# Embedding normalisation of a hybrid decoder step: from feature rows to token tiles, with eight PSUM banks for the transposes

## What is computed

```python
def layer_norm(x, g, b):
    xf = x.astype(jnp.float32)
    mu = jnp.mean(xf, -1, keepdims=True)
    var = jnp.mean(jnp.square(xf - mu), -1, keepdims=True)
    return ((xf - mu) * lax.rsqrt(var + LN_EPS) * g + b).astype(x.dtype)
...
xp = layer_norm(jnp.concatenate([meta, x_prompt], axis=1), emb_ln_g, emb_ln_b)
xs = layer_norm(x_sample, emb_ln_g, emb_ln_b)
...
proj = jnp.einsum('btd,dc->btc', x, w_in).astype(f32)      # first step of a layer's token mixer
```

## Time and profile before

| | us |
|---|---|
| runs before: median (lowest to highest of 3) | 1586.23 (1585.19 to 1592.24) |
| the profiled execution, its own time | 1596.57 |
| its span, first to last instruction | 1594.3 |
| TensorE busy | 1505.8 |
| VectorE busy | 923.2 |
| ScalarE busy | 686.4 |
| opening: start of the span to the first matmul of group 1 | 70.4 |

### The profile page before, as it was taken

The page is one execution under the profiler, slowest core; times in us unless marked ns, Lnnn a source line. Parts: engine busy times, 40 slices in busy tenths (PEclk is TensorE's granted clock), DMA queues, the critical chain, the costliest instruction groups (busy, mean ns, idle before and its releaser), DMA issues.

```text
span 1594.3 us, 30590 instructions
## 1 busy us (share of the span) xinstructions
PE 1505.8 (94%) x12047; PEld 1221.0 (77%) x12047; DVE 923.2 (58%) x1499; ACT 686.4 (43%) x1067; POOL 89.1 (6%) x86
## 2 busy tenths in 40 slices
PE   3899999999999999999989999999999999999995
PEld 2677878777788888878767887877777888887874
DVE  5767775546755555533476777555585555553334
ACT  4655552343743434322365555333264343432224
POOL 0011112110000000000001111111000000000000
PEclk7999999999999999999999999999899999999998
DMA  7222233221223222232333322321212323222321
GB/s 210 71 82 81 81 86 103 83 87 62 80 80 105 79 94 90 72 85 86 107 93 86 82 81 81 108 82 54 88 61 80 104 80 105 79 80 75 96 73 57
DMA packets 175042, 138.19 MB, mean 87 GB/s; under 512 B 5064, under 2 KB 169192, under 8 KB 174776
## 3 DMA queue, kind: packets, MB, share of 16 engines
q1 hardware_dynamic: 168192, 113.46, 23.8%
q0 software_dynamic: 5408, 18.60, 4.2%
q10 hardware_dynamic: 1372, 5.16, 0.9%
HBM read 125.12 MB, written 12.07 MB: 86 GB/s over the span
## 4 chain that ended last, share of the span: by engine, by line
PE 75%; DVE 10%; ACT 8%; DVEq 3%; issue 2%; ACTq 1%; DMA 1%; SPq 0%
PE ACC L561 62%; ACT X L973 2%; ACT XH L972 1%; PE OT L705 1%; PE SCR L735 1%; DVE Fb L1460 1%; PE OT L757 1%; DVE WL L1380 1%; PE SCR L618 1%; PE SCR L806 1%; DVE X L1430 1%; ACT WH L946 1%; PE SCR L561 1%; PE OT L561 1%; DVE B L1466 1%
## 5 line engine op out<-in xcount | busy, mean ns | idle before, releaser
L561 PE MATMUL ACC<-XH,WH 128*128 128x280 f16 x2304 | 483.6, 288 | 8.4 <-DVE XL L1435 6.6
L561 PE MATMUL ACC<-XL,WH 128*128 128x280 f16 x2304 | 483.1, 287 | 0.0
L561 PE MATMUL ACC<-XH,WL 128*128 128x280 f16 x2304 | 482.7, 287 | 0.0
L1380 DVE SCALAR_TENSOR_TENSOR WL<-stage,WH 128x2048 f16<-128x2048 f32 (+1 forms) x108 | 228.8, 2119 | 128.0 <-ACT WH L946 121.7
L561 PEld LDWEIGHTS ACC<-XH,WH 128*128 128x128 f16 x2304 | 227.8, 101 | 70.6 <-DVE XL L1435 8.4
L561 PEld LDWEIGHTS ACC<-XL,WH 128*128 128x128 f16 x2304 | 228.8, 99 | 54.4 <-issue 0.9
L561 PEld LDWEIGHTS ACC<-XH,WL 128*128 128x128 f16 x2304 | 229.1, 99 | 53.4
L946 ACT ACTIVATE WH<-stage 128x2048 f16<-128x2048 f32 (+1 forms) x108 | 190.5, 1764 | 98.4 <-PE ACC L561 71.9
L561 PE MATMUL ACC<-shared,WH 128*128 128x280 f16 x1320 | 214.7, 283 | 2.0 <-issue 2.0
L561 PEld LDWEIGHTS ACC<-shared,WH 128*128 128x128 f16 x1320 | 128.8, 98 | 31.2 <-issue 3.1
L561 PE MATMUL ACC<-shared,WL 128*128 128x280 f16 x660 | 139.8, 283 | 0.0
(11 more groups left out here) (262 smaller groups left out, 2004.0 us busy)
## 6 DMA issues: line engine op xcount, KB each, us to landing
stage<-in_w_in_dram SPq DMA_DIRECT2D x64, 512.0 KB, 5.3
stage<-in_w_a_dram SPq DMA_DIRECT2D x44, 512.0 KB, 4.3
stage<-in_w_b_dram SPq DMA_DIRECT2D x44, 512.0 KB, 4.4
stage<-in_w_down_dram SPq DMA_DIRECT2D x32, 384.0 KB, 3.5
stage<-in_w_down_dram SPq DMA_DIRECT2D x32, 320.0 KB, 3.9
out_dram<-shared POOLq DMA_DIRECT2D x16, 512.0 KB, 3.9
stage<-in_w_o_dram SPq DMA_DIRECT2D x16, 512.0 KB, 3.9
shared<-in_state_ret_dram POOLq DMA_DIRECT2D x8, 512.0 KB, 4.6
```

What stands on the lines that cost most here:

```text
L561: last = mm(dst(h), lhs, x[:, xk + k, tokens(h)], start=begin, stop=end)
L1380: stt(out=wl[:, 0:width], in0=stage[:, s, 0:width], scalar=W_SCALE, in1=wh[:, 0:width], op0=ALU.mult, op1=ALU.subtract).then_inc(w_lo[s], 1)
```

## The change

The first layer norm is computed on the token tiles as they lie, before the transposes. The three whole prompt tiles come in three DMAs, each with a semaphore of its own. For each tile VectorE takes mean and variance along the free dimension (`token_sums`: two `bn_stats` over 512 elements, one `bn_aggr`), ScalarE the deviation of one column (`token_deviation`), and VectorE normalises the tile in place (`token_norm`). TensorE transposes the normalised tiles into eight PSUM banks, one for each feature row (`left_bank`); all of ACC, OT and SCR are free at that time. Tiles 0 to 2 hold the left half. VectorE applies gain and bias straight out of the bank into X (`opening_rows`), ScalarE copies X to XH (`left_high`), VectorE makes XL as before.

The right half's transposes (tiles 2 to 4, `transpose_right`) are woven between the matmuls of the left half, into four banks used twice; ScalarE applies gain and bias out of these banks into XH and X (`right_rows`). The right half's matmuls, all four tiles, wait once for all eight XL pairs.

The squares, the reductions over feature rows, the matmuls with ones, and the mean and variance rows go away for these two halves; they stay for all later layer norms. The parameters are fetched in ten DMAs of norm parameters (both layers in one) and four of convolution parameters; the norm parameters are transposed ahead of tile 2, the convolution parameters with the last right row. ScalarE's function table is loaded ahead of all DMAs, and the large tables are fetched behind the deviation of the last tile. ScalarE's `split_hi` and VectorE's `split_lo` of the next unit keep their place in the program ahead of VectorE's last two XL pairs of the right half.

The diff, cut: without declarations of semaphores, index changes, and the removed bodies of `transpose_params`, `transpose_x`, `start_jobs` and `first_rows`:

```diff
+        SUM6, MEAN_VAR, RSD = (B[:, a:b] for a, b in ((0, 12 * TT5), (12 * TT5, 14 * TT5), (14 * TT5, 15 * TT5)))
...
+        def norm_column(n, o, m):
+
+            at = m + 8 * o if n == 0 else 16 + 32 * ((n - 1) % 2) + 16 * o + 8 * ((n - 1) // 2) + m
+            return par[:, 2 * P + at:2 * P + at + 1]
...
+        left_bank = (ACC[:, 0, 0, :], ACC[:, 1, 0, :], OT[:, 1, :], ACC[:, 0, 1, :], ACC[:, 1, 1, :], OT[:, 0, :], SCR[:, 0, :], SCR[:, 1, :])
+        right_bank = (OT[:, 1, :], ACC[:, 0, 1, :], ACC[:, 1, 1, :], SCR[:, 1, :]) * 2
+        norms_bank = SCR[:, 1, LEFT_TILES * P:LEFT_TILES * P + ROWS2]
+        conv_bank = SCR[:, 1, T - RIGHT0:T - RIGHT0 + DEPTH * ROWS01]
...
-            sp.dma_start(XT[:, 1:4, :], xp[first:first + 3 * P, :].rearrange("(i p) d -> p i d", p=P)).then_inc(x_in[1], 16)
-            sp.dma_start(XT[0:TAIL, 4, :], xp[first + 3 * P:SEQ, :]).then_inc(x_in[2], 16)
-            sp.dma_start(XT[TAIL:R5, 4, :], x_sample.rearrange("b t d -> (b t) d")).then_inc(x_in[2], 16)
+            for i in range(1, 4):
+                sp.dma_start(XT[:, i, :], xp[first + (i - 1) * P:first + i * P, :]).then_inc(x_in[i], 16)
+            sp.dma_start(XT[0:TAIL, 4, :], xp[first + 3 * P:SEQ, :]).then_inc(x_in[4], 16)
+            sp.dma_start(XT[TAIL:R5, 4, :], x_sample.rearrange("b t d -> (b t) d")).then_inc(x_in[4], 16)
...
-                    last.then_inc(scr_full, 1)
+            def transpose_left():
+
+                pe.wait_ge(consts_in, 16)
+                for i in range(LEFT_TILES):
+                    if i == LEFT_TILES - 1:
+                        pe.wait_ge(norms_in, 16 * N_NORM_DMAS)
+                        nc.tensor.transpose(norms_bank, rows[0:ROWS2, 2, :], ident[0:ROWS2, 0:ROWS2]).then_inc(norms_full, 1)
+                    pe.wait_ge(token_rows, i + 1)
+                    for m in range(KT):
+                        if i == LEFT_TILES - 1 and m == KT - 1:
+                            pe.wait_ge(norms_ready, 1)
+                        last = nc.tensor.transpose(left_bank[m][:, i * P:(i + 1) * P], XT[:, i, m * P:(m + 1) * P], ident)
+                        if i == LEFT_TILES - 1:
+                            last.then_inc(row_full, 1)
+
+            def transpose_right(m):
+
+                pe.wait_ge(x_ready, (2, 2, 3, 4, 5, 5, 6, 6)[m])
+                pe.wait_ge(token_rows, TT5)
+                for i in range(LEFT_TILES - 1, TT5):
+                    n, at_ = P if i < 4 else R5, i * P - RIGHT0
+                    last = nc.tensor.transpose(right_bank[m][:, at_:at_ + n], XT[0:n, i, m * P:(m + 1) * P], ident[0:n, 0:n])
+                if m == KT - 1:
+                    last.then_inc(ot_full, 2)
+                    pe.wait_ge(params_in, 16 * N_CONV_DMAS)
+                    for b in range(DEPTH):
+                        last = nc.tensor.transpose(conv_bank[:, b * ROWS01:(b + 1) * ROWS01], rows[0:ROWS01, b, :], ident[0:ROWS01, 0:ROWS01])
+                last.then_inc(row_full, 1)
+
+            def opening_units():
+
+                pairs = ((1, (acc(0), acc(1))), (2, (lambda h: OT[:, h, 0:HALF], lambda h: SCR[:, h, 0:HALF])))
+
+                def one(k, pair, h):
+                    for c in range(2):
+                        last = products(pair[1][c], pair[0], 2 * P, c * P, lambda _: k, XH, XL, k, 1, k == 0, k == KT - 1, (h,))
+                        if h == 1 and k == KT - 1:
+                            last.then_inc(acc_full, 1)
+
+                transpose_left()
+                pe.wait_ge(w_lo[0], 2)
+                for k in range(KT):
+                    if k % 2 == 0:
+                        pe.wait_ge(x_ready, k // 2 + 1)
+                    one(k, pairs[0], 0)
+                    for m in {4: (0, 1), 5: (2,), 7: (3,)}.get(k, ()):
+                        transpose_right(m)
+                pe.wait_ge(w_lo[1], 2)
+                for k in range(KT):
+                    one(k, pairs[1], 0)
+                    for m in {2: (4, 5), 5: (6, 7)}.get(k, ()):
+                        transpose_right(m)
+                pe.wait_ge(x_ready, 2 * PAIRS)
+                for pair in pairs:
+                    for k in range(KT):
+                        one(k, pair, 1)
...
-            for i in range(3):
-                transpose_x(i)
-            transpose_params()
-            norm_stats(0, 0, 1, jobs_at_start["left",][1])
-            for i in (3, 4):
-                transpose_x(i)
             for l in range(DEPTH):
-                first_group(l)
+                if l == 0:
+                    opening_units()
+                else:
+                    first_group(l)
...
+            nc.scalar.preload_act_table_set("natural_log_exp_and_others")
             act.dma_start(tab[:, 0:first_tables], consts[:, 0:first_tables]).then_inc(consts_in, 16)
-            loads = []
+            norms = [(emb_ln_g, 0), (emb_ln_b, 8), (ln1_g, 16), (ln1_b, 32), (ln2_g, 48), (ln2_b, 64),
+                     (hg_norm_g, ROW_HG), (rt_gn_g, ROW_RG), (rt_gn_b, ROW_RB), (lb_logits, ROW_LB)]
+            assert len(norms) == N_NORM_DMAS
+            for src, at_ in norms:
+                flat = src.rearrange("(k p) -> k p", p=P) if len(src.shape) == 1 else src.rearrange("l (k p) -> (l k) p", p=P)
+                act.dma_start(rows[at_:at_ + flat.shape[0], 2, :], flat).then_inc(norms_in, 16)
...
-            act.dma_start(tab[:, first_tables:n_const], consts[:, first_tables:n_const]).then_inc(tables_in, 16)
+                act.dma_start(rows[0:CONV_W * FT, l, :], conv_w[l].rearrange("j (f p) -> (j f) p", p=P)).then_inc(params_in, 16)
+                act.dma_start(rows[CONV_W * FT:ROWS01, l, :], conv_b[l].rearrange("(f p) -> f p", p=P)).then_inc(params_in, 16)
...
-            def first_rows(i):
+            def token_deviation(i):
                 n = P if i < 4 else R5
-                act.wait_ge(scr_full, jobs_at_start["x", i, 1][0])
-                f(X[:, 4:8, i * P:i * P + n], SCR[:, 0, :].rearrange("p (k t) -> p k t", k=4)[:, :, 0:n], ACT.Copy).then_inc(scr_read[0], 1)
-
-            def first_sums(h):
-                act.drain().then_inc(x_high_rows, 1)
-                act.wait_ge(x_low_rows, h + 1)
-                f(first_squares[:, :, tokens(h)], X[:, :, tokens(h)], ACT.Square).then_inc(first_sq, 1)
...
+                if i == 0:
+                    act.wait_ge(consts_in, 16)
+                act.wait_ge(token_var, i + 1)
+                f(RSD[0:n, i:i + 1], MEAN_VAR[0:n, 2 * i + 1:2 * i + 2], ACT.Ln, bias=tab[0:n, eps_at:eps_at + 1])
+                act.drain()
+                f(RSD[0:n, i:i + 1], RSD[0:n, i:i + 1], ACT.Exp, scale=-0.5).then_inc(token_rstd, 1)
+
+            def left_high(pair):
+                act.wait_ge(left_rows, pair + 1)
+                f(XH[:, 2 * pair:2 * pair + 2, tokens(0)], X[:, 2 * pair:2 * pair + 2, tokens(0)], ACT.Copy).then_inc(ln_out, 1)
+
+            def right_rows(pair):
+                for m in (2 * pair, 2 * pair + 1):
+                    act.wait_ge(row_full, KT + m + 1)
+                    src = right_bank[m][:, HALF - RIGHT0:T - RIGHT0]
+                    g, b = (norm_column(0, o, m) for o in range(2))
+                    f(XH[:, m, tokens(1)], src, ACT.Identity, scale=g, bias=b)
+                    last = f(X[:, m, tokens(1)], src, ACT.Identity, scale=g, bias=b)
+                last.then_inc(ln_out, 1)
+
+            for i in range(LEFT_TILES):
+                token_deviation(i)
+            act.wait_ge(norms_full, 1)
+            f(par[:, 2 * P:2 * P + ROWS2], norms_bank, ACT.Copy)
+            act.drain().then_inc(norms_ready, 1)
+            split_hi(0, 0, (acc_full, 1), slot=1)
+            for i in range(LEFT_TILES, TT5):
+                token_deviation(i)
+            act.dma_start(tab[:, first_tables:n_const], consts[:, first_tables:n_const]).then_inc(tables_in, 16)
+            for pair in range(PAIRS):
+                left_high(pair)
+                if pair == 1:
+                    split_hi(1, 0, (acc_full, 1), slot=2)
+            for pair in range(PAIRS):
+                right_rows(pair)
+            f(par[:, 0:DEPTH * P].rearrange("p (l c) -> p l c", l=DEPTH)[:, :, 0:ROWS01],
+              conv_bank.rearrange("p (l c) -> p l c", l=DEPTH), ACT.Copy)
             act.drain().then_inc(params_ready, 1)
-            first_sums(0)
-            split_hi(0, 0, (acc_full, 1), slot=1)
-            norm_mean(0, 0, ot0(0))
-            norm_rstd(0, 0, 0)
-            for pair in range(2):
-                norm_rows(0, 0, 0, pair)
-            for i in (3, 4):
-                first_rows(i)
-            first_sums(1)
-            for pair in range(2, PAIRS):
-                norm_rows(0, 0, 0, pair)
-            split_hi(1, 0, (acc_full, 1), slot=2)
...
+                if l:
+                    nc.scalar.preload_act_table_set("natural_log_exp_and_others")
+                    norm_mean(4 * l + 1, 1, ot0(l) + 1)
+                    norm_rstd(4 * l + 1, 2 * l, 1)
```

(72 more changed lines are left out.)

84 lines of the change are left out of this document (17 added, 67 removed).

## The result

| | before, us | changed, us |
|---|---|---|
| median of 18 runs each (lowest to highest) | 1593.06 (1585.19 to 1605.66) | 1583.73 (1576.65 to 1590.72) |
| ratio, with its 95% interval | | 0.9937 (0.9915 to 0.9958) |
| profiled execution, its own time | 1596.57 | 1584.03 |
| its span | 1594.3 | 1582.4 |
| first product of TensorE | 36.69 | 21.11 |

The change is faster by 0.63% by the ratio, 10.0 us of 1593, with an interval of 0.42 to 0.85% (the two medians lie 9.3 us apart). Yet the time, 1583.73 us, lies above the range of 1570 to 1583, because the level of the kernel before was taken from three runs that happened to be low.

What follows compares the result with a forecast made beforehand. The prediction took the opening's start-up chain across engines as the bound. Its end was 46.9 + 11.4 + 1.6 = 59.9 us against 70.4, 10.5 us earlier, so 1586.2 - 10.5 = 1575.7 us, range 1570 to 1583.

Steps and rivals of the forecast that it cites:

- What bounds the kernel: Opening group of four tiles: a start-up chain ending at 70.40 us; its earlier end, 10.5 us, is the whole gain.
- Fetches: Opening DMAs: separate token tiles land at 9.4, 10.9 and 12.5 us, first weights at 17 us with tables fetched later.
- VectorE's chain: Opening, VectorE: statistics 1.77 us per tile, normalising 0.87, rows 0.50; TensorE's first product at 23.2 us.
- TensorE to the end of the left half: Opening, left half: products and woven right-half transposes, from the fifth feature row at 29.7 us to 40.7 us.
- The pause: Before the right half: TensorE idles 6.2 us, until all eight XL pairs are ready at 46.9 us.
- The cold restart: Right half after the idle stretch: 14 matmuls at the low clock, 0.11 us more each, 1.6 us charged.
- 1 (longer VectorE chain): Opening, VectorE: the serial normalisation chain takes longer, up to 3.3 us, giving 1579.0 us, or 1582 with late tile; chance 0.15.
- 2 (late fetches): Opening DMAs: fetches land as late as before, giving 1580.8 us by weights or 1578.8 by tokens; chance 0.10.
- 3 (tables meet the second unit's weights): Opening DMAs: the delayed tables hold up the second unit's weights and the right half, up to 1586.2 us; chance 0.03.
- 4 (TensorE cold throughout): Opening, TensorE: low clock from 29.7 us on, 1593.6 us, chance 0.05; only the left half cold, 1584.6, chance 0.04.
- How the numbers follow: Whole kernel: likeliest 1575.7 us, range 1570 to 1583; faster 0.65, same 0.28, slower 0.07.

Runs made afterwards that it cites:

- e2_one_token_dma: The changed kernel with token tiles 1 to 3 fetched in one DMA with one semaphore again; ratio to the kernel before 0.9944.
- e5_busy_pause: The changed kernel with 50 unused identity transposes in TensorE's pause before the right half; ratio to the kernel before 0.9927.
- e7_stats_twice: The changed kernel with every tile's two bn_stats done a second time, result unused; ratio to the kernel before 0.9965.
- e1_tables_early: The changed kernel with the large tables fetched right behind the parameters again, ahead of ScalarE's first work; ratio to the kernel before 0.9976.
- e4_xl_by_pair: The changed kernel with the last two XL pairs ahead of the next unit's low weights and TensorE waiting pair by pair; ratio to the kernel before 0.9897.
- e3_xl_first: The changed kernel with the last two XL pairs ahead of the next unit's low weights, still one wait for all eight; ratio to the kernel before 0.9906.

## Why the prediction came out as it did

**What bounds the kernel, and that the gain is counted at the start of group 1**: right. Nine runs move that point by what was expected within 1.2 us. What lies behind it was put at nothing, and rightly as far as can be seen: 1521.6 us, inside the 1517.0 to 1527.9 of the three executions with the old arithmetic.

**Fetches**: right in kind, too cautious in size. Tile 0 let VectorE start at 6.14 us (7.1 predicted), tile 1 was there by 7.8 (9.4), the weights by 15.5 (17). By the fit of the Trainium skill (DMA: Bandwidth & Descriptors, section Anatomy of one DMA — SWDGE (gpsimd) path; the prediction names the section Bandwidth, which has the advice on 1 MiB), an estimate for tile 1 was 10.3 us if each transfer paid its fixed part in turn. That fit is for DMAs issued by GpSimd, and these are issued by SyncE; the trace shows the tile by 7.83 us, and the one large transfer only at 11.81 (e2_one_token_dma). Here it counts more that a semaphore fires for the part that is wanted first than that the transfer is large.

**VectorE's chain**: right. bn_stats 0.68 us (0.69 taken from the copy), normalising 0.81 (0.87), a row 0.57 (0.50), aggregation 0.21 (0.17). First product at 21.1 us (23.2), k 4 at 27.3 (29.7): 2.4 us early: 1.0 from the first landing, 0.6 from the second, and the rest from steps that follow one another a little faster than their single durations.

**TensorE to the end of the left half**: mis-sized, by 2.2 us. From k 4 to the last product I had 11.0 us; it took 13.2 (27.26 to 40.47). 72 matmuls at 0.119 are 8.6, so the transposes cost 4.6 instead of 2.4. The chain shows why: three transposes take 0.41 or 0.56 us, not 0.27, and six products right behind them 0.82 us against 0.71 in group 1 (that the shorter third piece, of 48 tokens, makes the difference is my reading and was not tried). My row for four equal transposes in a row did not hold for pieces of two sizes between matmuls.

**The pause**: 6.05 us, 6.2 predicted, for the reason given. **The cold restart**: mis-sized. I charged one 3.24 us stretch, 1.6 us; it lasted 5.43 us and cost 2.65 by e5_busy_pause. The restarts of these runs were not equally long: behind a pause of 6.04 to 6.05 us the first 48 products took 7.77 us in e7_stats_twice, 8.53 in the changed kernel and 8.66 in e1_tables_early, against 5.72 without a pause (e4_xl_by_pair), so the one that I read was no constant. The end of the opening is the sum, 60.77 against 59.9, and that the two are so near is in part luck: k 4 came 2.4 us early, the left half behind it took 2.2 us too long and the right half 1.25 (14.25 against 13.0).

**The rivals.** 1 (longer VectorE chain): no, although e7_stats_twice shows that it would have counted in full. 2 (late fetches): no, but e1_tables_early shows what it hung on, 5.95 us. 3 (tables meet the second unit's weights): no; the next copy had its weights when ScalarE came to it at 40.92. 4 (TensorE cold throughout): no. The wait of 1.36 us before k 4 (1.63 in e2_one_token_dma) left the clock at 1.00 from 27.3 to 40.5 us, with matmuls 0.12 us apart, and it fell again only in the pause. The rule of the Trainium skill (TensorE: Matmul & The Clock Gate, section HAM oscillation — how this bites in real kernels), that bursts between waits for data pay the low clock, agrees for the 6.05 us pause. The waits of that page's example are several microseconds long, so the waits of 1.4 and 1.6 us here, which left the clock alone, do not speak against it.

**How the numbers follow**: this is the step that failed. "1586.2 - 10.5" took the median of three runs for the level, and the range allowed "one us of measurement on either side". The difference was right, 10.0 us measured against 10.5 (in part by the luck told above); the level was 6.8 us off, 1593.06 us over 18 runs, and the range missed the time by 0.7 us. Three runs that lie 7 us apart already say that the level is not known to 1 us, and the profiled execution, 1596.57 us, stood 10 us above their median. Why executions differ so much stays open. "Faster by over 0.5%" at 0.65 was borne out by the centre of the ratio, though the interval reaches down to 0.42%.

## What to carry to other kernels

When an opening is one chain through several engines, look for the fetch that its new order will ask for earlier and clear the way for it in the same change: the arithmetic alone gave 4.7 us, the late tables alone nothing, and the arithmetic with both fetch edits 9.6. Read where a wait for "all" stands behind unrelated work in another engine's program: moving two small operations ahead of one large one gave 8.3 us more (e3_xl_first), some two thirds as the idle stretch (6.05 us down to 0.59) and a third as the clock that fell in it (2.65). Give a forecast as a difference, and put the scatter of the runs, not a guess, around the level.

## What was not expected of the hardware

- Early in a trace a recorded clock of 1.00 need not be the clock that TensorE has: in e7_stats_twice the first products, at a recorded 1.00, came 0.23 us apart, the distance that goes with a recorded 0.50 in the earlier trace rows, and the transposes of the earlier trace rows took 0.236 us each against the 0.11 of the earlier trace rows.
- A cold restart after nearly the same pause lasted 3.90 us in one kernel and 5.43 us in another.
- Executions of one program on the same kind of chip differ by some 1.3% (1585.19 to 1605.66 us), with the first 70 us repeating within 0.6.
